# Another order for the side work of the second block's two layers, in a one-core transformer kernel

## The reference, cut to what matters

```python
proj = jnp.einsum('bsd,de->bse', x, w_in[layer])            # 1024 -> 14400 columns
z, xbc, dt_raw, dq, dk, dv, dg, cq, cg, gl = jnp.split(proj, splits, axis=-1)
y_ssd = _ssd_branch(z, xbc, dt_raw, ...)     # conv of 5 taps + silu, chunked scan both ways
o = _diff_attention(q, k, v, lam)            # 8 heads, two softmaxes each
oc = _memory_cross_attention(cq, mem_kv)     # 4 heads over 256 memory tokens
merged = gates0 * (y_ssd @ w_br_ssd) + gates1 * (y_diff @ w_br_diff) + gates2 * (y_cross @ w_br_cross)
x = _layernorm(ALPHA * x + merged @ w_out[layer], ln_g[layer], ln_b[layer])
```

## Time and profile before

| | |
|---|---|
| median of 3 runs | 4009.11 us (4002.52 to 4012.85) |
| time of the profiled execution | 4009.11 us, with a span of 4007.2 us |
| PE busy | 3820.4 us, 95% of the span |
| DVE busy | 2623.7 us, 65% |
| ACT busy | 1561.4 us, 39% |
| POOL busy | 182.0 us, 5% |
| mean granted TensorE clock | 0.972 |
| layer 0 of the second block | about 1740.7 to 2881 us |
| layer 1 of the second block | about 2881 to 4007.2 us |

### The profile page before, as it was taken

How to read it: one execution, slowest core, us unless ns; L and a number is a source line. 1 busy time by engine, 2 the same in 40 slices (tenths; PEclk the granted TensorE clock), 3 DMA queues, 4 the chain that set the end, 5 groups by cost and what they waited for, 6 DMA issues and landing times.

```text
span 4007.2 us, 49615 instructions
## 1 busy us (share of the span) xinstructions
PE 3820.4 (95%) x19548; PEld 3135.5 (78%) x19548; DVE 2623.7 (65%) x4164; ACT 1561.4 (39%) x2629; POOL 182.0 (5%) x335
## 2 busy tenths in 40 slices
PE   6989999998999999999999999999999999999998
PEld 5769878887789788888876788677888877886776
DVE  6887455556785522446878843786668888537865
ACT  3453332234542422333443343553334433335532
POOL 0000000000000000001111000000001120000010
PEclk9989899999998999989999999999999999999999
DMA  7502156532211332324455233133244453321233
GB/s 242 169 22 85 69 170 207 191 105 95 64 48 53 109 103 81 105 95 127 151 158 152 74 95 95 48 116 128 83 142 149 140 175 96 95 90 53 82 133 111
DMA packets 227128, 451.60 MB, mean 113 GB/s; under 512 B 18560, under 2 KB 63648, under 8 KB 225104
## 3 DMA queue, kind: packets, MB, share of 16 engines
q1 hardware_dynamic: 197584, 335.12, 25.9%
q0 software_dynamic: 29312, 113.32, 9.0%
HBM read 412.45 MB, written 35.93 MB: 112 GB/s over the span
## 4 chain that ended last, share of the span: by engine, by line
PE 78%; DVE 13%; ACT 4%; DMA 2%; issue 2%; POOL 0%; SPq 0%; DVEq 0%; ACTq 0%; POOLq 0%
PE ps L608 60%; PE ps L151 13%; PE ps L162 4%; DVE arena L173 3%; DVE spl L173 3%; ACT arena L247 2%; DVE arena L188 2%; DVE sm L194 1%; DMA arena<-cumd 1%; ACT sph L247 1%; DVE X L173 1%; DMA arena<-kvd 1%; PE ps L859 1%; PE ps L157 1%; DVE arena L224 0%
## 5 line engine op out<-in xcount | busy, mean ns | idle before, releaser
L173 DVE TENSOR_TENSOR spl<-ring,sph 128x1024 fp32r<-128x1024 f32 (+2 forms) x556 | 650.4, 1178 | 662.7 <-ACT sph L247 661.6
L247 ACT ACTIVATE sph<-ring 128x1024 fp32r<-128x1024 f32 (+2 forms) x556 | 558.7, 1019 | 717.0 <-PE ps L608 690.6
L608 PE MATMUL ps<-sph,HTh 128*128 128x512 f32 (+3 forms) x1680 | 656.9, 391 | 13.4 <-DVE HTl L173 5.0
L608 PE MATMUL ps<-spl,HTh 128*128 128x512 f32 (+3 forms) x1680 | 619.2, 369 | 0.0
L608 PE MATMUL ps<-sph,HTl 128*128 128x512 f32 (+3 forms) x1680 | 618.6, 368 | 0.0
L247 ACT ACTIVATE arena<-ps 128x512 f32<-128x512 f32 (+2 forms) x570 | 314.0, 563 | 742.1 <-PE ps L608 432.8
L608 PE MATMUL ps<-HTh,sph 128*128 128x512 f32 x1360 | 539.5, 397 | 11.3 <-ACT X L247 10.5
L608 PE MATMUL ps<-HTh,spl 128*128 128x512 f32 x1360 | 531.2, 391 | 0.0
L608 PE MATMUL ps<-HTl,sph 128*128 128x512 f32 x1360 | 531.2, 391 | 0.0
L151 PE MATMUL ps<-arena 128*128 128x128 f32 (+6 forms) x2264 | 372.6, 343 | 43.4 <-ACT arena L247 12.3
L608 PE MATMUL ps<-sph 128*128 128x512 f32 x992 | 399.8, 403 | 5.1 <-DVE spl L173 5.1
(11 more groups left out here) (218 smaller groups left out, 4901.5 us busy)
## 6 DMA issues: line engine op xcount, KB each, us to landing
ring<-in_w_in SPq DMA_DIRECT2D x264, 512.0 KB, 3.8
arena<-in_ada_w SPq DMA_DIRECT2D x88, 512.0 KB, 5.0
arena<-cumd POOLq DMA_DIRECT2D x128, 256.0 KB, 3.9
ring<-in_w_down SPq DMA_DIRECT2D x44, 512.0 KB, 3.7
ring<-in_w_gate SPq DMA_DIRECT2D x40, 512.0 KB, 3.7
ring<-in_w_up SPq DMA_DIRECT2D x40, 512.0 KB, 4.1
ring<-in_w_mem SPq DMA_DIRECT2D x32, 512.0 KB, 3.4
ring<-in_w_out SPq DMA_DIRECT2D x32, 512.0 KB, 3.6
```

The costliest lines, as they stand in the source:

```text
L173: self.e.tensor_tensor(o, a, b, op).then_inc(*self.done.up())
L247: self.e.activation(o, a, f, **kw).then_inc(*self.done.up())
L608: ins = pe.e.matmul(o, l, r, start=k0 == 0 and i == 0 and not b.pairs, stop=k0 + b.ks == b.kt and i == 3 * b.ks - 1 and (c0 > 0 or not b.p ...
```

## The change

Only the two strings of the second block's layers are replaced, `("proj", 0)` and `("proj", 1)`. Both hold the same letters in the same numbers as before: 625 `M`, 81 `p`, 72 `s`, 61 each of `c` and `d`, 38 `f`, 33 `t`, 11 `n`, 10 `g`, 7 each of `x` and `y`, 5 each of `z` and `m`, and in layer 1 5 `r`. The steps of each stream keep their order among themselves; what changes is between which main steps they stand. In layer 0 the first two `s` move from main steps 22 and 30 to 73 and 81; in layer 1 the second `s` moves from 89 to 30, and the first four `r` from 5, 5, 17 and 26 to 20, 21, 23 and 23.

```diff
--- before.py
+++ after.py
@@ -55,23 +55,23 @@
         "ag2ag2agag2a3gagmihimhim4Mi2MhMiMhihiMihiMihiMi2MihiMiMhiMhihiMhihMhMi3MiMihi3MhihihihiMih3M2i2Mi2hM"
         "iMi2MiM2i3M2ib25M",
     ("proj", 0):
-        "22Ms8Msd4M2d2McMcMcMd2Mc2Md5M2c5Md3Mc2dc3Md5Mc2dMc2dM2dcMc2Mcd2Mc3Md14M2c3Mc2McMdcMdsMdsd3c2MdMcdM2s"
-        "5Md5McsMdc2Md6McdcMd4Mc2MdMc2dMc2Md2Mcs2MsdMscdsMdMd4Ms2McMdMdMs3MdMc2McMd2s2Mc3McdMs2Md6Mcs3McMcdsc"
-        "dc2ds3Mc2Md3McMsdsc2Mc3Mdc4Ms4cMdMcMcscdMd2Md3M3dsMsdcMc2MsdM2c2Mc2Mc2dMdcs2M2sMsMs3MsMs4M2s2M2s3MsM"
-        "sMp3MsM2pMsM2psp3Ms3Mp2spsMp4Mps2MpMpM3ps2p2M2spMpMspMsMspMs2Ms2Mp2Mp2Msp2Mpsp2s5M3p2sMp3Mp2sMpMspMp"
-        "M2s2p2MsMspMpMsM2p2s2pMpM2p5Mpg3p2M4pM2p2MpMpM2pMpMpM2p2M3p2MgMpgM3p2MpM2p3MpM4pM3p4Mg19Mg4Mg4MgMg5M"
-        "g4MtMt2MtMt4Mg2MtM3tMt2Mt2M2t3Mt2Mt2M2t3Mt5Mt5MtMt2Mt2Mt2Mt3MtMt5Mt4Mt2Mt3Mt30M3t6Mt7Mf2M2f2MfMf5MfM"
-        "2f2MfMf3Mf2Mf2MfMf3MfMfMfMfMf5MfMfMnfMf2M2f5Mn2Mf4MfMf3MnMf4Mf4MnMn2f2Mf2M2fM3fnxMnxyxMxyMxn2yxny2n"
-        "7M2yx4M2z2Mz2Mz4Mz29Mm12Mm2Mmsm3Mm28M",
+        "35McMdMd3Md8Md3M2d2Md2Mc4McMdc2Mcdc7M5c2M2dMcMsMcd2Mc5MscMdM2dMcdMdMc3Md6M2cMsdc2MdsMc4Mc2dcd2Mc2M2c"
+        "MsMcd5MscMd2Mcd4Ms2Md2MdMcdcMs2Mc3MscMcsc2M2ds2dMcMs2Mc2dc7Md3MsMd6MdMc2M2cdMdc2Ms2Msd4Mcs2MsdMd2Md"
+        "3MdMcsd2cMd2Md6Ms2cMd2Md2Msd3csc2dMc2MsMc2MscMdMdMdcMdcds2McMs2Msc2Ms2M2dc3McdsMsMsMsM2s2MsMsMs3Ms3M"
+        "sMsMsMp2M2p2sp3MpsM2p2M2sp3Mpsp3Mps2M2pMsp2MspsM2p2Ms2p2MpMsMs3Msps3MpMpsM2pMps2M2p2s2Mps2Mps2M2s2Mp"
+        "2Mpsp2Msp2sp2sMpMpMs2pMpsM2p2Mp2M2p2MpM2pM3p2MpM3pg2M3pMp2M2pMg3MpM2p2M3pMpM3p2M2p2Mp2Mpg3pM3p19Mg4M"
+        "g6MgMg3Mgt3Mt5Mt3M2t2Mt2Mt2Mtgt8Mt2Mt3MtM4tMt4M2t5M2t2M2t15Mt7MtMt5Mt7Mt10MtM2t15M2tg3MfM2f2Mf2Mf4Mf"
+        "2Mf3MfMf3MfM2f2Mf2Mf3MfsMf3MfMf3MfMf2Mf2Mf6MnMn4MfMn4Mf4Mn2f2Mn2fMfMf3MfMf3Mf2M5fMnxnMxy2x2Mnyx2yxny"
+        "2n3MyMy6Mx3Mz3MzM2z6Mz24MmMm15Mm3M2m27M",
     ("proj", 1):
-        "5M2r12Mr3Ms6Mr5Md4Mc7Mc3Mdc6MdMc2MdMcM2c2MdMc2Mc3Md3MdMd2Mdc2Md2c2M2dMd3Mc3M2c5Md3M2d2csc2MdMc3Mc3Md"
-        "MdsMcMcdMdMsc3Ms3McdMd4MdMsd3MdMd2c3Mc2Mc3McdMcsd2cds2dcs5MdscMc3McsMcMd3Mscs6MdMs5Ms3d3Ms2d3Msd2sdc"
-        "McdMc4Msd3McMdMsd8MdMcMscMcMcMc2Mds3McMcMc2dcdMcMdMdsMc2dMdcMcd2MsdMcMsMcMdM3csMc2dsMs2M2s8MsMsMsMs"
-        "3M2s5M2s2p3MspMpsMpM2psMpMs2p2M2sMp2M2s2p6Msps2MpMpspMs2MpMsMpMrp3Mps2M2p2M2sp2MpMspMsM2p2Mp2s2M2p4M"
-        "sps3MpM2s2pMp2MpspsMpMs2ps8M4s2p2M2pM5pg3p2Mp3M2pg2pMpM3p5M2pMpM2pgpM3p2M2pgM5p2M3p14Mg7Mg5Mg9MgMt3M"
-        "t2MtMt4Mt2M3t4Mt4MtMt7M3tMtMt9Mgt3MtMt3M3t2Mt11MtMt2MtMt7MsM3t7Mt8Mg2Mt11Mt7M3f3Mf4Mf2MfMf2MfMfMf2Mf"
-        "MfMf2MfMfMf2MfMf2Mf2MfMf3Mnf4Mf5Mn2Mf4Mf3Mn2Mf3Mf2MfMf2MfMfn3MfnM2f3Mf3M3f2nx2MyMxnyx2ynx2n4Myx2My"
-        "10MxMyMx2M3zM2z26M2m17M2m4Mm25M",
+        "17Ms3MrMr2M2r7Msd6Md7MdMc6Mc3MdcMcMc2McMdcd2McMd5Md2MdM2cd3M2cd6Md3MdMcd2M2dcMcdMd2c5Md2McMc3Mc2d2sM"
+        "dMd3M2cMd3Mc5Msc2Mdc2Mdc6MsMdMc3Mdcd2M2dc2MdscMdsdcsdcMcMs3MscMdsMsc5MdMcMsc9McMcd2MdMdMd4McMcs2McMs"
+        "dMcd2Md4M2cs3MdcMcd4MsMsMcMd4M2csMdMc3d2Ms2MdM3cdsd2cMs2M2c2McdMsdcs2d4MsdMs2M2dc2Ms2M2sMsM2s2M2s4Ms"
+        "Ms4MsMspMspsMpMps2MsMpM2p2M3pMpM2s4MsMsp2M2pspMpMpMsMs2ps3Mps2Mps2MspMs2Mp4MpMpMpMspspMp2sp2Ms2ps3Ms"
+        "psMp2M2pMspMpMp2spMspM2s2M2s3p2Mp4Mp2M2pMpMpMpM2pMpgpM4p2MpMg2p2M2pMpM2p2Mp3M2pMpg2MpMpgMpMpM4pM2p9M"
+        "g14Mg2Mg5Mg5Mt2Mt2Mt3Mt5MgtM2t6MtMt4MtMstM2t5MtM2tMtMt3MgMt6MtM2t3Mt3Mt4MtMt3Mt17M2tMt8Mt4Mt13Mt3MfM"
+        "2f2Mf2Mf4Mf2M3f2Mf2Mf3MfMf3MfMf2Mf2Mf3MfMf2Mf4Mf2Mf8M2n2Mf2Mn2Mf5Mf4Mn2fMfMf2Mn2fMfMf2MfMfMfM2fxnyxy"
+        "2MnMn2y2x3n2MyMxMy2Mx3MyMx2Mr2zMz4MzMz30M2m16M2m3Mm26M",
 }
```

## The result

The changed kernel takes 4047.99 us against 4010.98, medians of 4 runs each. The kernel is slower by 37 us, outside the predicted range. The profiled execution took 4049.31 us, 40.2 more than that of before.

The account below looks back on a forecast made before the run. PE was taken as the bound, side-work order able to win only its 71.4 us idle and clock losses; -2.1 - 3.3 + 5.8 + 2.2 + 1 + 1 + 1.2 = +5.8 on 4009.1 gave 4015 us, range 3996 to 4028.

Parts of the forecast that it names:

- rival 1: Layer 1's close rows put DVE behind and layer 0's gains don't come: +18 us, 4027; chance 0.22.
- The step that failed: Row spacing from main step 236 on: -3.3 us in layer 0, +2.2 us in layer 1.
- the row loop: Layer 0's scan: copy, issue and load of each row take 5.85 us, 29.25 for five rows against 24.0 of PE work.
- Its deficit less 1.4 to 4.3 us: Price of a tight group of rows: how far the loop falls behind PE's work, less 1.4 to 4.3 us.
- Rows of layer 1, 205 to 235: Layer 1, these main steps: closer rows cost 6.5 and 1 us, against 1.7 now, so +5.8 us.
- the three close rows: Layer 1, rows at main steps 213, 214 and 215: DVE 9.2 us behind, costing 4.9 to 7.8 us, taken as 6.5.
- Rows of layer 0: Layer 0's new row spacing: -2.1 us in main steps 208 to 235, -3.3 us in 236 to 289.
- The clock: Starts of both layers, main steps 1 to 16: between -5 and +5 us, taken as 0.
- Convolution, attention, `kvd`, switches: Layer 0's uncovered convolution tile +1 us, denser attention units +1, `kvd` loads unchanged, PE's 15 more switches +1.2.
- Rival 2: Layer 0's scan waits fall from 13.9 us to layer 1's 2.1, its start gets the better clock: -15, 3994; chance 0.17.
- Rival 3: Everything is hidden by the cover of 12 main steps, losses and gains cancel: 4010 us; chance 0.17.
- Rival 4: Loads of rows are shorter where spaced, a loop of 4.25 us takes 5 us from the sum: 4010; chance 0.06.

Follow-up runs that it names:

- 19 letters apart: Changed kernel with 8 `s` and 11 `p` of layer 1's string moved by one to three main steps, all behind main step 233: 4042.1 us, ratio 1.0070.
- 0.43 us less for each of 16 main steps: Changed kernel without the multiplication by 0.5 ending each silu eviction of dg and cg, 16 DVE operations per layer: 4040.8 us, ratio 1.0069.
- the second buffer: Second buffer for the reverse row: in the changed kernel from row 13 on, 4029.45 us, 1.0057; in the kernel before from row 14 on, 0.9998.
- the rows apart: Changed kernel with 10 letters `s` of layer 1's string moved so that rows 12 to 18 stand farther apart: 4044.1 us, ratio 1.0088.
- `p` alone: Changed kernel with only layer 1's letters `p` back where the kernel before has them, the scan's letters `s` new: ratio 1.0120.

## Why the prediction was wrong, point by point

The forecast was 4015 and the same; it is 4048. The kind of cause was right (the order in the scan, in layer 1, PE waiting for DVE) and rival 1 named the layer. The sizes and the mechanism behind them were not.

**The step that failed** is the price of the letters from main step 236 on. I priced only rows, by their spacing and their loads: +2.2 in layer 1 and -3.3 in layer 0, and the passing's letters `p` had no term. Measured, layer 1's waits from 241 to 289 rose by 11.7 us, and of these the loads hold 0.2. They come from products met one to two main steps behind the DVE step that feeds them, with other steps queued on DVE between: 19 letters apart halve them, and 0.43 us less for each of 16 main steps lowers them by 4. The queue itself is shown at one place, 7.6 us at main step 276; for the others it is argued from these two kernels. In the profile before I had read layer 0's 9.3 us of such waits as the row loop too; the second buffer leaves them but for 0.8 us (8.0 to 7.2 from main step 241 on), the other layer's layout removes them. That was the wrong inference at the root: a wait of DVE's behind a load was taken for the cause of all of PE's.

The price of the loop was misread too. I set its 5.3 us against 3.9 that PE had paid, but 3.15 of these ended at 2065.12, ahead of the first copy of the five rows (2065.77) and 5.7 us ahead of the first addition that waited for a load (2070.81). DVE up to there:

```profile
2063.66 0.69 DVE L173 TENSOR_TENSOR arena<-arena,sm 128x512 f32<-128x512 f32 x1
2064.38 0.69 DVE L173 TENSOR_TENSOR arena<-arena,ps 128x512 f32<-128x512 f32 x1
2064.99 0.68 DVE L173 TENSOR_TENSOR arena<-arena 128x512 f32<-128x512 f32 x1
```

No idle time is marked at these, and from 2048 us up to them DVE has only four waits, each of 0.7 us and for ACT. So this wait, one of the two largest in layer 0's scan, was none of the loop's, and of the 3.9 us only 0.7 can be. "Its deficit less 1.4 to 4.3 us" rests on the wrong wait.

**Rows of layer 1, 205 to 235: +5.8.** Measured 11.5 - 1.7 = +9.8 (to main step 241), and 8.8 - 1.7 = +7.1 in the kernel with layer 1's string alone. The term's bounds, 4.9 to 7.8 and 0 to 2.1 less the 1.7 of before, allow +3.2 to +8.2. But the term came near by luck: the waits at the three close rows are the same with two buffers, with the rows apart the sum is as large, and with the loads out of the way 7.7 us still stand.

**Rows of layer 0: -2.1 and -3.3.** Measured +5.2 in all (19.1 against 13.9). I had compared spacings of rows and not what stands between them.

**The clock.** I allowed it for the two starts, 0 with 5 us either way; these and the first block do vary by as much and more between executions of one string, 6.2 and 16 us. What I left out is the clock inside the scan: the grant there was 1.00 in layer 1 before and is 0.97 after, some 5.6 us in 187, and in the kernel with the longest stretch (`p` alone) it is 0.94.

**Convolution, attention, `kvd`, switches: +1, +1, 0, +1.2.** PE's waits for ACT at line 151 fell, from 5.6 + 6.0 to 4.3 + 2.5, and `kvd` in layer 0 from 4.3 to 2.1, where I had said rise and stay. At line 162, PE's waits for ACT rose in layer 0 from 1.9 to 3.8 and for line 188 fell from 1.2 to 0.6; in layer 1 those for line 188 rose from 0.8 to 4.1. Outside the stretch layer 1's waits rose by 2.6 us in all (24.1 in the layer, 21.5 in the stretch). The kernel with layer 1's old convolution, scan and passing, at 1.0007, shows that the new attention part costs nothing there; no kernel tests the new convolution alone. The switches, 15 x 0.08 us, are too small for any run here to tell.

**The rivals.** Rival 1 (4027, chance 0.22) had layer and sign; its price came from the loop alone and was 20 us short, and where its three close rows stand, main steps 211 to 215, lie 4.9 of the 24.0 us. Rival 2 was false for this change, for the new layer 0 isn't like layer 1. As a kernel of its own, with layer 1's string in both, it takes 3990 us, where rival 2 said 3994; of its waits' 11.8 us 11.2 came (13.9 to 2.7), the 4.8 of a better clock at layer 0's start did not (a grant of 0.50 in the profiled execution), so the nearness of the sum is part luck. Rival 3 fell with the 24 us. Rival 4 fell as well: 128 loads of a row land in 3.9 us at the median after, as before, and in 4.0 where all rows stand well apart. The Trainium skill (DMA: Bandwidth & Descriptors, the fit in the part on the fixed cost) would give about 2.6 us, an estimate from that page; the loads of rows in no kernel here agree with it.

What stays open: of the 21.5 us more of waits in the stretch, the buffer and the 19 letters together account for 10.9, and of the 32.7 us that layer 1 lost behind main step 16 for 13.8. The rest went only with the old layout of `s` and `p`; I take it for the same kind of wait at the spots that I didn't move, and haven't shown it place by place. Open too is why the medians give the buffer 18.5 us.

## What to carry to other kernels

Where an order of steps is written out, a product is safe only if the main steps ahead of it cover all that its operand's engine has queued at that point, in every stream, and that of the engines which that engine waits for; count the queue, not the spacing of one stream. An engine that is 80% busy over a stretch can be what nearly every wait there is for. When a wait in a profile has a vivid cause, remove that cause alone before you price other waits with it. And a layer that runs well next to one with the same work is a layout to copy: it gave 20 us here.

## What was not expected of the hardware

Waits of PE that are short cost clock as well. In the stretch after, the grant is 0.50 (1.2 GHz) from 3225.2, from 3266.2 and from 3365.2 us, within 1.2 us behind the ends of waits of 1.6, 2.9 and 2.8 us; behind waits of up to 2.1 us elsewhere in the stretch it stays at 1.00. Over the stretch the mean grant is 0.99 to 1.00 in every kernel with 0.6 to 2.8 us of waits in it, and 0.94 to 0.98 in those with 11.7 us or more, but not in their order: 0.96 with 11.7 us, 0.98 with 18.7, 0.97 with 24.0, 0.94 with 23.4.

And the same first 16 main steps of a layer run at a mean grant of 0.50 in one execution and 0.70 in another, 23.6 or 17.4 us, with PE busy all the time in both; the first block differs by up to 16 us between executions. In a comparison of single executions a difference under 20 us has to be placed in a stretch before it means anything.
